# Expert stage of a two-layer transformer step: 16 base tiles and 9 overflow tiles replaced by 10 full tiles and 8 passes of two 64-row halves

## The chip, the cores and the metric

The kernel runs on one core of a Trainium2 chip. The metric is device time in microseconds (us). One execution of the kernel before was also recorded by the hardware profiler; every number of the trace below is from it. Engines are called as in the profile: PE is TensorE (PEld its weight load), DVE is VectorE, ACT is ScalarE, POOL is GpSimd, SP is SyncE, which here only issues DMAs.

## The reference

640 tokens (128 of a prompt, 512 of a sample) of width 1024 go through two layers. Each layer is attention of two kinds, gates and an output projection, and then a mixture of experts, all in float32. The part that the change touches is this:

```
scores = sigmoid(h @ w_router); sel = scores + b_router         # 16 experts in 4 groups
best   = the group whose two highest sel have the largest sum
idx    = top_k(sel inside that group, 2); w = scores[idx] / sum
out   += w * ((silu(h @ w_gate[e]) * (h @ w_up[e])) @ w_down[e])   # for both experts e of a token
```

w_gate[e] and w_up[e] are 1024x256, w_down[e] is 256x1024: 3.15 MB for one expert, 50.3 MB for the 16 of a layer. There are 2 x 640 = 1280 (token, expert) rows a layer. On the inputs that setup_inputs() draws, the reference gives these rows per expert (counted with the reference itself in float32):

```
layer 0:  76  68  88  84  55  98 112  91  75  73  65  87  48  88  73  99
layer 1:  46  13  48  31  92 153  71 104  90  41  48 115 102 112 109 105
```

## The kernel before

Each engine has its own instruction stream, written out by hand, and semaphores (class Signal) tie them together. A layer runs attention, projections, the output projection w_out, the router with its matmuls (router(t)), a block of small DVE operations that turn the scores into a place for each row (L1566 to L1618), and the expert stage. 

**Tiles.** The expert stage works in tiles of 128 rows. MOE_TILES is 25 in each layer, whatever the routing: 16 base tiles, tile e for the first 128 rows of expert e, whose weights are known ahead, and N_OVER = 9 overflow tiles for what an expert has beyond 128 rows; the expert of an overflow tile stands in etab, computed from the routing, and an unused overflow tile loads and computes expert 15's weights with rows that aren't stored. SCHED is base 0, over 0, then base, base, over, seven times, and last base, over. PE runs all 25.

**Matmuls.** In a base tile every product is done in three passes (pass3, L1792 to L1794): weights and rows are split into a high part (ACT, L809, written as fp32r) and the rest (DVE, L1157), and hi x hi, lo x hi and hi x lo are accumulated. Gate and up together are 8 x 3 matmuls of 128x512, down is 4 x 3. An overflow tile does gate and up in plain float32 from the raw data (L2128, 8 matmuls; the profile shows each float32 matmul as two records) and down in three passes, after the split of its two down units (L1064, L1539).

**PE's order** for tile n: gate_up(n); x_transposes(n + 1) (L2105, 8 transposes of the gathered rows); down(n - 1); hid_transposes(n) (L2156). After tile 0 come slot_weights (L2163, L2166), which place the routing weights. gate_up(n) waits for the rows' split (L1625), for its weights, and for PSUM bank 0, which the silu and the product of tile n - 1 read.

**DMA.** Expert weights come in six units of 512 KB from w_moe. SP issues them: weights(n, first, last) at L600 for base tiles, in 2 x 6 slots that alternate by expert, and over_weights(j) at L607 for overflow tiles, in 6 slots. Each load waits until PE has used its slot. The first base tile's six units and four of the second's are issued during w_out and the router, among the loads of the next layer's modulation weights (head_pair, raw_h). The others follow etab. POOL issues the gathers of rows, rows(n) at L765 (xg from h2_d by the indices inv_i, two buffers, two tiles ahead), and the scatters of results, store_rows(n) at L780 (ye_d from ysb by row_i). Both are indirect DMAs with a bounds check: an index beyond it is skipped. POOL's queue is in order: a gather behind a scatter waits until it is issued.

**Around it.** Before rows(0) can be gathered, the DVE block must have given inv_i (L1613). PE meanwhile runs head_pair matmuls of the next layer (layer 0 only, L1765: four matmuls side by side, each 32 output columns wide in the array, as at L1751 for mod_pair and L1720 in the prologue) and keep_busy matmuls (L1700). The neighbourhood attention's na_values (L2004) uses 64-column matmuls, two side by side. After the last tile SP loads ye_d back (L567) and DVE adds it up with the gates gt, which POOL had loaded at the end of the w_out stage; in layer 0, ACT and DVE also split the next layer's first weight units (L813, L1161), which SP loads into slots 0 to 5 as soon as the last even expert has left them.

## Time and profile before

| | |
|---|---|
| median of 3 runs | 1751.56 us (1748.84 to 1753.78) |
| profiled execution, span from first to last instruction | 1758.7 us |
| instructions | 22838 |
| PE busy | 1654.2 us, 94% |
| DVE busy | 1087.9 us, 62% |
| ACT busy | 859.0 us, 49% |
| POOL busy | 207.0 us, 12% |
| DMA | 368.02 MB, mean 209 GB/s |

A time of the profiled execution other than its span isn't given; the span lies 7.1 us above the median. Busy shares are averages over stages: PE's 94% says that it is nearly always the engine at work, and the slices say where DMA comes close to its most. A matmul's record covers its latency, so consecutive records overlap; the distance of two starts is what a matmul costs.

### The profile page before, as it was taken

The numbers are of one execution on the slowest core, as the hardware profiler recorded it, in microseconds if no ns is written. First come the engines' busy times: TensorE is split into PE (matmuls) and PEld (weight loads), VectorE is DVE, ScalarE is ACT, GpSimd is POOL, SyncE is SP. The second block draws the span as 40 slices with busy tenths as digits, with TensorE's granted clock in tenths as the row PEclk, the third lists the DMA queues.
The fourth block names the chain that finished last, engine by engine and source line by source line (L and its number), as shares of the span: only waits on it lengthen the run. The fifth ranks groups of instructions, "written<-read, shape, count | busy, mean of one in ns | idle before, by whom it ended". The sixth has DMA issues, their size and how long they took to land. (4 is left out here: it accounts for less than half of the span.)

```text
span 1758.7 us, 22838 instructions
## 1 busy us (share of the span) xinstructions
PE 1654.2 (94%) x8536; PEld 1255.2 (71%) x8536; DVE 1087.9 (62%) x1917; ACT 859.0 (49%) x1537; POOL 207.0 (12%) x257
## 2 busy tenths in 40 slices
PE   4999999999999999999779999999999998999992
PEld 2777777777887677777467677777778886777771
DVE  2476655345564668787676566544655476878775
ACT  4534553355422357676553445344552233767661
POOL 1000000011100112222100000001110001222210
PEclk9999999999999999999989999999999999999996
DMA  8531234434636699999635411453436536899975
GB/s 342 211 126 43 72 106 161 148 108 153 217 127 270 250 338 355 382 353 371 218 141 185 172 42 61 146 200 107 154 105 207 215 115 233 313 380 356 385 295 207
DMA packets 106780, 368.02 MB, mean 209 GB/s; under 512 B 20384, under 2 KB 20448, under 8 KB 106160
## 3 DMA queue, kind: packets, MB, share of 16 engines
q1 hardware_dynamic: 76752, 279.48, 43.3%
q0 software_dynamic: 29776, 84.48, 13.7%
q10 hardware_dynamic: 144, 2.62, 0.4%
q8 instruction: 68, 1.11, 0.3%
q14 instruction: 40, 0.33, 0.1%
HBM read 347.03 MB, written 49.45 MB: 225 GB/s over the span
## 5 line engine op out<-in xcount | busy, mean ns | idle before, releaser
L1157 DVE TENSOR_TENSOR lo<-raw,hi 128x1024 fp32r<-128x1024 f32 x298 | 352.2, 1218 | 104.4 <-ACT hi L809 104.2
L1792 PE MATMUL ps<-hi,hT_hi 128*128 128x512 f32 x960 | 395.2, 412 | 5.5 <-ACT o_a L1012 3.0
L1794 PE MATMUL ps<-hi,hT_lo 128*128 128x512 f32 x960 | 378.8, 395 | 0.0
L1793 PE MATMUL ps<-lo,hT_hi 128*128 128x512 f32 x960 | 377.8, 394 | 0.0
L809 ACT ACTIVATE hi<-raw 128x1024 fp32r<-128x1024 f32 x298 | 299.3, 1054 | 138.9 <-DMA raw<-w_stream 135.5
L1792 PEld LDWEIGHTS ps<-hi,hT_hi 128*128 128x128 f32 x960 | 183.1, 191 | 63.5 <-issue 18.6
L1794 PEld LDWEIGHTS ps<-hi,hT_lo 128*128 128x128 f32 x960 | 182.4, 190 | 41.0
L1793 PEld LDWEIGHTS ps<-lo,hT_hi 128*128 128x128 f32 x960 | 183.5, 191 | 33.4
L2128 PE MATMUL ps<-over,xT 128*128 128x512 f32 x288 | 126.6, 592 | 0.0
L1792 PE MATMUL ps<-hi,xT_hi 128*128 128x512 f32 x256 | 103.3, 404 | 0.5 <-DVE xT_lo L1625 0.3
L780 POOL DMA_INDIRECT ye_d<-ysb,row_i x50 | 57.4, 1147 | 371.2 <-DVE ysb L1637 335.0
L1794 PE MATMUL ps<-hi,xT_lo 128*128 128x512 f32 x256 | 100.1, 391 | 0.0
L1793 PE MATMUL ps<-lo,xT_hi 128*128 128x512 f32 x256 | 100.0, 390 | 0.0
L2128 PEld LDWEIGHTS ps<-over,xT 128*128 128x128 f32 x288 | 53.3, 190 | 60.3 <-issue 60.3
L989 ACT ACTIVATE e_da<-ps,neg_m 128x640 f32<-128x640 f32 (+1 forms) x80 | 55.9, 705 | 71.6 <-DVE neg_m L1416 71.5
L1416 DVE TENSOR_REDUCE neg_m<-ps 128x1 f32<-128x640 f32 (+1 forms) x80 | 53.7, 712 | 56.9 <-PE ps L1933 38.4
L1272 DVE TENSOR_REDUCE ssum<-sq 128x8 f32<-128x512 f32 x40 | 27.3, 685 | 83.1 <-ACT stg L906 83.1
L905 ACT ACTIVATE sq<-ps 128x512 f32<-128x512 f32 x40 | 23.9, 598 | 109.3 <-PE ps L1794 109.3
L1108 ACT ACTIVATE silu_g<-ps 128x256 f32<-128x256 f32 x50 | 19.2, 384 | 108.9 <-PE ps L1794 76.2
L845 ACT ACTIVATE pT_na<-ps 128x384 f32<-128x384 f32 (+1 forms) x80 | 31.8, 447 | 78.9 <-PE ps L1784 78.8
L765 POOL DMA_INDIRECT xg<-h_d,inv_i x50 | 57.0, 1141 | 71.9 <-DVE inv_i L1613 31.9
L1099 ACT ACTIVATE ysb<-ps,w_slot 128x512 f32<-128x512 f32 x50 | 34.4, 688 | 58.8 <-PE ps L1794 58.8
(290 smaller groups left out, 2871.4 us busy)
## 6 DMA issues: line engine op xcount, KB each, us to landing
raw<-w_moe SPq DMA_DIRECT2D x192, 512.0 KB, 6.8
raw<-w_stream SPq DMA_DIRECT2D x112, 512.0 KB, 4.3
over<-w_moe SPq DMA_DIRECT2D x108, 512.0 KB, 7.8
raw_m<-w_stream SPq DMA_DIRECT2D x70, 512.0 KB, 5.3
bias_na<-na_bias POOLq DMA_DIRECT2D x32, 384.0 KB, 3.3
sg<-sg_d POOLq DMA_DIRECT2D x8, 1280.0 KB, 9.8
y<-ye_d SPq DMA_DIRECT2D x20, 512.0 KB, 7.4
raw_p<-w_stream SPq DMA_DIRECT2D x16, 512.0 KB, 16.2
```

Source lines behind the costliest of these rows:

```text
L765: po.indirect_dma_start(xg[n % 2][:], None, h2_d, bass.IndirectOffsetOnAxis(inv_i[:, XD_COL[n]:XD_COL[n] + 1], 0), bounds_check=NT * P - 1 ...
L780: po.indirect_dma_start(ye_d, bass.IndirectOffsetOnAxis(row_i[:, XD_COL[n]:XD_COL[n] + 1], 0), ysb[n % 2][:], None, bounds_check=2 * NT * ...
L809: act.activation(hi[s][:], raw[s][:], ACT.Copy).then_inc(is_hi.sem, 1)
L845: act.activation(dst, src, ACT.Copy, scale=scale).then_inc(tr_act.sem, 1)
L989: act.activation(e_da[:, i % 2, m, 0:nk], ps_flat[:, m * 1024:m * 1024 + nk], ACT.Exp, bias=neg_m[:, 2 * (i % 2) + m:2 * (i % 2) + m + 1], ...
L1099: act.activation(ysb[n % 2][:, 0:512], ps[:, 2, :], ACT.Copy, scale=w_slot[:, c:c + 1]).then_inc(y_act.sem, 1)
L1157: dve.tensor_tensor(lo[s][:], raw[s][:], hi[s][:].bitcast(F32), ALU.subtract).then_inc(is_lo.sem, 1)
L1416: dve.tensor_reduce(neg_m[:, c:c + 1], ps_flat[:, m * 1024:m * 1024 + nk], AX.X, ALU.max, negate=True).then_inc(mx_done.sem, 1)
L1792: pe.matmul(out, w_hi, m_hi, start=first, stop=False)
L1793: pe.matmul(out, w_hi, m_lo, start=False, stop=False)
L1794: return pe.matmul(out, w_lo, m_hi, start=False, stop=last)
L2128: ins = pe.matmul(ps[:, 0, :], xT[:, kc, :], over[k][:, j * 512:(j + 1) * 512], start=(kc == 0), stop=(kc == KC - 1))
```

## The change

Rows of an expert are cut in chunks of 64. Chunks go in pairs into full tiles of 128 rows; a rest of one chunk becomes a half. There are N_FULL = 10 full tiles and N_HALF = 16 halves in N_PAIR = 8 pairs: 18 tiles in each layer instead of 25. Full tiles are given out in the order of the experts until the 10 are used, and what is left goes into halves. By the counts above, layer 0 has 14 experts that need a full tile, of which 10 get one, and 10 halves; layer 1 uses 10 full tiles and 7 halves. A used half comes first: halves 0 to 9 are pairs 0 to 4, halves 0 to 6 are pairs 0 to 3.

- Full tiles are as the base tiles before, with the expert taken from etab (weights(j, units)); full tile 0 does gate and up in plain float32 from the raw data, like an overflow tile before. No weights are loaded before etab is known.
- A pair is one tile whose rows 0 to 63 are of one expert and 64 to 127 of another. Gate and up are 8 x 2 float32 matmuls, each with 64 of the rows as its 64 columns in the array and 512 moving columns, the two halves to the two halves of PSUM's partitions; down is 2 x 2 x 2 of them. Nothing of a pair is split in hi and lo.
- POOL loads a pair's weights by indirect DMA with indices eidx: pair_gate_up(q), 2 x 2.1 MB (128 rows of 16 KB each), once PE has done gate_up of the pair before, since there is one buffer for each half; pair_down(q), 4 x 0.5 MB, once down of the pair before is done. An empty half's indices are out of bounds.
- The schedule is full 0, pair 4, full 1, pair 0, full 2, pair 5, full 3, pair 1, full 4, pair 6, full 5, pair 2, full 6, pair 7, full 7, pair 3, full 8, full 9.
- The DVE block has more steps before the places are known: two counts instead of one, two running sums over the experts instead of one, what is kept of the full tiles, and the tables of the experts, which now come before the places.
- The weight tensors are laid out anew: w_gu has one row of 16 KB for each (layer, expert, partition), w_dn one of 4 KB for each (layer, half of the inner width, expert, partition).
- Two of the loads of gt move behind the last pair's down, since their place is lent to pair_dn.

```diff
-N_OVER = (2 * NT * P) // (P + 1)
-MOE_TILES = N_EXP + N_OVER
+HALF = P // 2
+CHUNKS = NT * P // HALF
+N_HALF = N_EXP
+N_FULL = -(-(N_EXP + (2 * NT * P - N_EXP) // HALF - N_HALF) // 2)
+N_PAIR = N_HALF // 2
+MOE_TILES = N_FULL + N_PAIR
+PAIRS = [i + h * (N_PAIR // 2) for i in range(N_PAIR // 2) for h in (1, 0)]
+for _j in range(N_FULL):
+    SCHED += [("full", _j)] + [("pair", i) for i in PAIRS[_j:_j + 1]]
+IS_PLAIN = [not full or n == 0 for n, full in enumerate(IS_FULL)]
...
+                def weights(j, units):
                     e = sp.value_load(etab[0:1, j:j + 1], min_val=0, max_val=N_EXP - 1)
+                    for k in units:
+                        w = mslot(j, k)
+                        sp.wait_ge(used[w].sem, used[w].at(l, mload(j, k) - 1))
+                        src = gu_rows[l, e, :, k * D:(k + 1) * D] if k < 4 else dn_rows[l, k - 4, e]
+                        sp.dma_start(raw[w][:], src.rearrange("p (a b) -> p a b", b=512)).then_inc(loaded[w].sem, 16)
+                for p in range(4, KC):
                     head_pair(p)
                 sp.wait_ge(etab_ready.sem, etab_ready.at(l, 0))
-                sp.wait_ge(h2_stored.sem, h2_stored.at(l, NT - 1))
+                weights(0, range(MU))
                 if l + 1 < DEPTH:
+                    for b in (1, 2):
+                        sp.wait_ge(h_used[b].sem, h_used[b].at(l, 1))
+                sp.wait_ge(xg_loaded[0].sem, xg_loaded[0].at(l, 0))
+                weights(1, range(MU))
                 for n in range(MOE_TILES):
+                    if IS_FULL[n] and SCHED[n][1] + 2 < N_FULL:
+                        weights(SCHED[n][1] + 2, range(4))
+                    if n >= 1 and IS_FULL[n - 1] and SCHED[n - 1][1] + 2 < N_FULL:
+                        weights(SCHED[n - 1][1] + 2, (4, 5))
...
+                def pair_gate_up(q):
+                    if q >= 1:
+                        po.wait_ge(gu_used.sem, gu_used.at(l, q - 1))
+                    for h in range(2):
+                        c = 2 * PAIRS[q] + h
+                        po.indirect_dma_start(pair_gu[h][:], None, w_gu, bass.IndirectOffsetOnAxis(eidx[:, 0, c:c + 1], 0),
+                                              bounds_check=(l + 1) * N_EXP * P - 1, oob_is_err=False
+                                              ).then_inc(gu_loaded.sem, 16)
...
                 rows(0)
+                if l + 1 < DEPTH:
+                    for b in (0, 2):
+                        po.wait_ge(h_used[b].sem, h_used[b].at(l, 1))
+                po.wait_ge(eidx_ready.sem, eidx_ready.at(l, 0))
+                pair_gate_up(0)
                 rows(1)
...
                 for n in range(MOE_TILES):
                     if n + 2 < MOE_TILES:
                         rows(n + 2)
+                    if n in PAIR_AT[:-1]:
+                        pair_gate_up(PAIR_AT.index(n) + 1)
                     if n >= 1:
                         store_rows(n - 1)
+                    if n == 1:
+                        pair_down(0)
+                    if n - 1 in PAIR_AT[:-1]:
+                        pair_down(PAIR_AT.index(n - 1) + 1)
...
+                RED(chunks[:], counted[:, :, 0:CHUNKS], AX.X, ALU.add)
+                after(chained(RED(fulls[:], counted[:, :, CHUNKS:], AX.X, ALU.add)))
+                before(fulls, f_base)
+                after(chained(TS(kept[:], f_base[:], -1.0, float(N_FULL), ALU.mult, ALU.add)))
+                after(chained(STT(out=kept[:], in0=kept[:], scalar=0.0, in1=fulls[:], op0=ALU.max, op1=ALU.min)))
+                after(chained(STT(out=chunks[:], in0=kept[:], scalar=-2.0, in1=chunks[:], op0=ALU.mult, op1=ALU.add)))
+                before(chunks, h_base)
...
+                    if kind == "pair":
+                        pe.wait_ge(gu_loaded.sem, gu_loaded.at(l, 2 * PAIR_AT.index(n) + 1))
+                        for kc in range(KC):
+                            for h in range(2):
+                                cs = slice(HALF * h, HALF * h + HALF)
+                                ins = pe.matmul(ps[cs, 0, :], xT[:, kc, cs], pair_gu[h][:, kc * 512:(kc + 1) * 512],
+                                                start=(kc == 0), stop=(kc == KC - 1))
+                        ins.then_inc(gu_used.sem, 1)
+                        return
```

## Rows read from the trace of the kernel before

**Rows 1.** A stretch of layer 0's expert stage: busy us, granted clock, DMA share, GB/s.
```profile
core 0: us, PE busy (x) PEld busy (x) DVE busy (x) ACT busy (x) POOL busy (x), PEclk, DMA share, GB/s
700.00:780.00 80.00, 80.00 (x354) 59.44 (x353) 61.68 (x73) 55.89 (x80) 19.40 (x18) 1.00 0.96 370
```
**Rows 2.** PE's timeline, start and us: first transposes and last matmul of each stage.
```profile
615.52 1.42 PE L2105 MATMUL ps<-ident,xg 128*128 128x128 f32 x8 [1.84 <-DMA xg<-h_d,inv_i]
...
868.30 0.39 PE L1794 MATMUL ps<-over_hi,hidT_lo 128*128 128x512 f32 x1
...
1476.90 1.97 PE L2105 MATMUL ps<-ident,xg 128*128 128x128 f32 x8 [3.45 <-DMA xg<-h_d,inv_i]
...
1728.36 0.39 PE L1794 MATMUL ps<-over_hi,hidT_lo 128*128 128x512 f32 x1
```
**Rows 3.** PE's timeline across three tiles in the middle of layer 0.
```profile
673.54 1.03 PE L2105 MATMUL ps<-ident,xg 128*128 128x128 f32 x8
...
682.95 1.03 PE L2105 MATMUL ps<-ident,xg 128*128 128x128 f32 x8
...
686.79 7.03 PE L2128 MATMUL ps<-over,xT 128*128 128x512 f32 x16
693.66 1.04 PE L2105 MATMUL ps<-ident,xg 128*128 128x128 f32 x8
```
**Rows 4.** PE's timeline: matmuls of 32 columns, four side by side, and what follows.
```profile
35.67 1.92 PE L1720 MATMUL ps<-raw_p,c_act 128*32 128x512 f32 x16
...
945.48 0.39 PE L1794 MATMUL ps<-hi,hT_lo 128*128 128x512 f32 x1
945.80 1.06 PE L1751 MATMUL ps<-raw_m,c_act 128*32 128x512 f32 x8
946.80 0.50 PE L1792 MATMUL ps<-hi,hT_hi 128*128 128x512 f32 x1
947.13 0.39 PE L1793 MATMUL ps<-lo,hT_hi 128*128 128x512 f32 x1
```
**Rows 5.** PE's timeline: matmuls of 64 columns, two side by side.
```profile
403.61 0.66 PE L2004 MATMUL ps<-pT_na,v_sh 128*64 128x128 f32 x8
...
404.42 0.88 PE L1784 MATMUL ps<-ident,p_na 128*128 128x128 f32 x6
```
**Rows 6.** DVE's timeline: scores to places, layer 0, and the last step in layer 1.
```profile
602.25 0.23 DVE L1585 TENSOR_TENSOR nb<-ps,rc 128x64 f32<-128x64 f32 x1 [0.52 <-PE ps L2084]
...
603.23 0.42 DVE L1590 TENSOR_REDUCE base_s<-nb 128x16 f32<-128x256 f32 x1
...
604.43 0.24 DVE L1594 TENSOR_TENSOR slot<-slot,rc 128x80 f32<-128x80 f32 x1
...
608.84 0.18 DVE L1613 TENSOR_SCALAR inv_i<-ps 128x25 int32<-128x25 f32 x1 [0.39 <-PE ps L2093]
...
1466.92 0.18 DVE L1613 TENSOR_SCALAR inv_i<-ps 128x25 int32<-128x25 f32 x1 [0.38 <-PE ps L2093]
```
**Rows 7.** Line L765 (ns min/median/max; us to landing), and PE's timeline of filler matmuls before them.
```profile
L765 POOL DMA_INDIRECT xg<-h_d,inv_i x50: 985/1106/2114, 609.9 to 1696.9; - x50
...
DMA to landing us min/median/max: 3.3/7.8/9.3
...
603.07 4.15 PE L1700 MATMUL ps<-rope_c,ident 128*128 128x256 f32 x18
```
**Rows 8.** DMA queues by packets, MB and share of 16 engines; DMA issues, us to landing.
```profile
q0 software_dynamic: 29776, 84.48, 13.7%
...
bias_na<-na_bias POOLq DMA_DIRECT2D x32, 384.0 KB, 3.3
...
x<-x_in POOLq DMA_DIRECT2D x1, 2560.0 KB, 13.4
x_spill<-x POOLq DMA_DIRECT2D x1, 2560.0 KB, 9.8
...
tok<-tok_in POOLq DMA_DIRECT2D x1, 5.0 KB, 9.6
```

More of the change, by code:

```diff
@@ L446, in program @@
         etab_ready = Signal("etab_ready", 1)
+        eidx_ready = Signal("eidx_ready", 1)
         half = [(MOE_TILES + 1 - b) // 2 for b in range(2)]
@@ L1590, in _ @@
-                after(chained(RED(base_s[:], nb[:], AX.X, ALU.add)))
-                after(chained(STT(out=base1[:], in0=base_s[:], scalar=float(P), in1=con["c15"], op0=ALU.mult, op1=ALU.add)))
-                after(chained(STT(out=slot[:], in0=place, scalar=float(P), in1=bc_t(base1[:]), op0=ALU.is_ge, op1=ALU.mult)))
+                counted = nb[:, :, 0:CHUNKS + CHUNKS // 2]
+                after(chained(TT(counted, total.unsqueeze(2).to_broadcast([P, N_EXP, CHUNKS + CHUNKS // 2]),
+                                 con["steps"].unsqueeze(1).to_broadcast([P, N_EXP, CHUNKS + CHUNKS // 2]), ALU.is_gt)))
@@ new lines, in _ @@
+                for i, (c0, c1) in enumerate(((0, N_FULL), (N_FULL, N_FULL + N_HALF))):
+                    ins = TT(ecmp[:, c0:c1, :], con["iota_t"][:, c0:c1].unsqueeze(2).to_broadcast([P, c1 - c0, N_EXP]),
+                             ends[:, i, :].unsqueeze(1).to_broadcast([P, c1 - c0, N_EXP]), ALU.is_ge)
+                after(chained(ins))
+                after(chained(RED(etab_f[:], ecmp[:], AX.X, ALU.add)))
+                TS(etab[:], etab_f[:, 0:N_FULL], float(N_EXP - 1), None, ALU.min).then_inc(etab_ready.sem, 1)
@@ new lines, in gate_up @@
+                    for k in range(4):
+                        w = mslot(i, k)
+                        if IS_PLAIN[n]:
+                            pe.wait_ge(loaded[w].sem, loaded[w].at(l, mload(i, k)))
+                        else:
+                            pe.wait_ge(is_lo.sem, is_lo.at(l, msplit(i, k)))
+                        for j in range(2):
+                            kc = 2 * k + j
+                            if IS_PLAIN[n]:
+                                ins = pe.matmul(ps[:, 0, :], xT[:, kc, :], raw[w][:, j, :], start=(kc == 0), stop=(kc == KC - 1))
+                            else:
```

332 lines of the change are left out of this document (154 added, 178 removed).

## The prediction

> **What bounds the kernel now.** I read the table of stretches first: in the middle of the expert stage of layer 0 PE is busy for 80.00 of 80 us at the full clock (2.4 GHz), while DMA stands at a share of 0.96 and 370 GB/s [rows 1]; layer 1 is alike. So PE sets the pace, and DMA is so near its most that whatever shortens PE meets it. Then PE's timeline gives the length of the two stages, from the first transposes to the last matmul: 868.69 - 615.52 = 253.2 us in layer 0, 1728.75 - 1476.90 = 251.9 us in layer 1 [rows 2]. The distance of the transposes of neighbouring tiles is the price of a tile: 9.41 us for a base tile, 10.71 us for one with an overflow tile's float32 gate and up [rows 3]. 16 x 9.41 + 9 x 10.71 = 247 us, which leaves 5 to 6 us for the two ends: the stage is the sum of its tiles, with no stall in it. The time to be won or lost is therefore 25 tiles against 18, at prices that PE sets, as long as the weights come in time.
>
> **The price of a tile in parts.** The overflow tile's gate and up take 693.66 - 686.79 = 6.87 us, 0.859 us for each of 8 float32 matmuls [rows 3]. A base tile has 24 passes in their place and costs 1.30 us less, so a pass is 5.57 / 24 = 0.232 us, and what is neither gate, up nor down is 9.41 - 36 x 0.232 = 1.06 us.
>
> **A pair.** It has 12 rounds (8 for gate and up, 4 for down) of two float32 matmuls in different halves of the array's columns. Before has four such matmuls side by side, 32 columns each: one round of four takes 1.06 us, two rounds 1.92 us [rows 4], so a round costs 0.86 us, as much as one full-width float32 matmul. They run at the same time. Going in and out of this mode costs 0.09 + 0.11 + 0.10 = 0.3 us beyond the matmuls' own (945.48 to 945.80 is 0.32, 945.80 to 946.80 is 1.00 against about 0.89, 946.80 to 947.13 is 0.33, with 0.23 normal) [rows 4]; a pair does it twice. Pair: 12 x 0.86 + 0.6 + 1.06 = 12.0 us. No row shows two 64-column float32 matmuls that stream 512. The nearest are na_values': 12 passes with their weight loads in 0.81 us [rows 5], at most 0.07 us a load, 0.27 us a round if none were hidden. So a pair lies between 12.0 and 12.0 + 12 x 0.27 = 15.2; I take 12.0, since in the rounds of four the loads were hidden. The Trainium skill (TensorEngine Tiling (Array Packing), Key Properties) says that changing the tiling mode drains the engine, which speaks against a stage that changes it four times a pair; the 0.3 us above is that drain as this trace has it, so the rule is in the sum already.
>
> **PE's sum.** Of 16 base tiles 9 remain as full tiles, and full 0 costs what an overflow tile costs. Gone are 7 base tiles and 8 overflow tiles, new are 8 pairs: -7 x 9.41 - 8 x 10.71 + 8 x 12.0 = -55.6 us a layer, -111 us for both.
>
> **DVE, ACT, POOL.** Splits fall from 114 to 56 units a layer, by the code, so DVE and ACT have more room than before in tiles that are as long. POOL issues per full tile and pair 4 gathers and scatters and 6 weight loads. Its cost for an indirect load of 16 KB rows isn't shown; an indirect DMA of 4 KB rows takes 1.1 us of POOL [rows 7], and even with four times that for the two of 16 KB rows the cycle's POOL work is 8 x 1.1 + 2 x 4.4 = 17.6 us of 21.4. Empty halves load nothing, if indices out of bounds are skipped: the software queue moved 84.48 MB, its direct DMAs (34 groups of issues, first and last shown) come to 63.5 MB, and the remaining 21.0 MB are just 2 x 2 x 1280 rows of 4 KB; the unused rows of 25 tiles moved nothing [rows 8].
>
> **The start of the stage.** The DVE block gets longer before the places are known. By size, 25 elements cost 0.18 us, 80 cost 0.24, 256 cost 0.42 [rows 6], about 1 ns for each further element, and 0.04 between two. Before, the eight steps from the count to slot took 604.67 - 602.25 = 2.4 us [rows 6]. After there are 24: ten of 16 elements (1.8), four of 256 and two of about it (2.5), four of 80 (1.0), a reduction of 416 (0.6), two counts (0.6), 160 compared (0.3), and gaps (0.8), 7.6 us in all. That is +5.2, and -0.2 for smaller tables. inv_i (609.0 in layer 0 [rows 6]) moves to about 614.0. This is on the path. What follows gets shorter: a gather takes 3.3 us at least and 7.8 in the median [rows 7], and it now meets only the loads of full 0 (3.1 MB, begun some 6 us earlier, as etab comes first) instead of a full queue. PE had its first rows 6.5 us after inv_i in layer 0 and 9.8 us in layer 1 [rows 2, 6]; I expect 5 in both. PE's filler ends at 607.2 [rows 7] and would wait until 612.6 for the places; after such an idle stretch (3.45 us) the eight transposes took 1.97 us instead of 1.04 [rows 2, 3], so about 1 us more. Together +5 us for both layers (3 to 8). No weights are preloaded now, but full 0's start at etab (about 607.7) and take 8.5 us at 370 GB/s, so that they are there at about 617, before its rows: nothing; at two thirds of that rate 3 us are lost, the upper end of the 8.
>
> **DMA.** Full tiles 31.5 MB, halves 31.5 MB in layer 0 and 22 MB in layer 1, rows 10.5 MB: 73.5 and 64 MB against 89 before. At 0.37 MB/us [rows 1] that is 199 and 173 us, beside 197.6 us of PE (253.2 - 55.6). So it fits on average, barely in layer 0; what matters is when. Gate and up of a pair have one buffer. Its 4.19 MB can start when PE is through with gate_up of the pair before and are wanted a cycle less that gate_up later: 9.41 + 12.0 - 8 x 0.86 = 14.5 us. POOL's big direct DMAs took 9.8 and 13.4 us for 2.62 MB [rows 8]; 4.19 MB at those rates are 15.7 and 21.5 us, so 1 to 7 us are missing. The wait stands on PE before gate_up; behind it are the transposes, down and thus ys of the tile before. This occurs only for pairs that are loaded and not the first: 4 in layer 0, 3 in layer 1 (pair 3 there has one half, 2.1 MB, which fits). I take 2 us, the rate of the quicker row, since every second pair is empty and leaves the queue idle: 7 x 2 = 14 us (7 to 49). Layer 0's first pair is loaded too, with rows(1) behind it in POOL's queue and full 1's 3.1 MB beside: 7.9 MB from about 617 end at 638, gate_up of full 0 at about 628. If POOL's go first, 6 us are lost, between 0 and 11. Such idle stretches cost PE its clock for a moment, about half a us each and more after the longest: 4 us (0 to 10).
>
> **The end.** SP can load the next layer's first six units only once full 8 has left slots 0 to 5, 16 to 9 us before the last matmul; 3.1 MB are 8.5 us. Nothing, by this cover. The last tile ends as before.
>
> **Sum.** 1758.7 - 111 + 5 + 14 + 6 + 4 = 1676.7 us of span; the profiled execution lies 7.1 us above the median, so 1669.6: I say 1670. The low end leaves out all stalls and takes 3 for the start, 1643; I put it at 1640. The high end has 49 + 11 + 10 of stalls and clock, 8 for the start, and a third of the unhidden loads (1 us a pair, 16): 1758.7 - 111 + 94 - 7.1 = 1735.
>
> **The rivals.**
> First, *the queues share alike*. In the 14.5 us SP also has 1.05 MB (down units) and 2.1 MB (gate and up of a later full tile) to load, none of it urgent. If the indirect load gets no more than its equal part, it ends when all 7.3 MB are moved, at 0.37 MB/us 19.8 us: 5.3 us missing, 7 x 3.3 = 23 us more than I take, and some 4 more at the start of layer 0: 1697. For it speaks that in before a gather of 0.5 MB took 7.8 us in the median [rows 7] beside SP's loads; against it, that the 16 KB rows may weigh more than SP's 4 KB rows, and that SP's queue is empty half the time. The Trainium skill (DMA: Bandwidth & Descriptors, Queues, rings and completion order) says that each DMA engine goes round between its queues packet by packet, which with packets of equal size is this rival. Chance 0.22.
> Second, *no two at once*. If two 64-column float32 matmuls don't run side by side, a pair costs 24 x 0.859 + 0.6 + 1.06 = 22.3 us, 16 x 10.3 = 165 us more, with the load waits hidden (-24): 1670 + 165 - 24 = 1811, slower. It decides from 18.6 us a pair, where 8 pairs and 2.5 us of start make up for the 7 x 9.41 + 8 x 10.71 = 151.6 us that go. Four 32-column ones do run together [rows 4]; only the width is new. 0.07.
> Third, *the indirect loads are slow*. If the software queue can't do better than a gather and a scatter in 7.8 us (1.05 MB, 0.134 MB/us [rows 7]), gate and up take 31 us and 17 are missing each time; with down's 2.1 MB and the rows in the same queue two cycles need 63 us instead of 43: 1670 + 20 x 7, with layer 0's start 20 instead of 6 and the 14 already in my sum taken off, 1810, slower. Against it: the direct DMAs of the same queue [rows 8]. 0.08.
> Fourth, *a mixture worse than my bounds* (slow issue on POOL, the clock, late units of full tiles), 1735 to 1760: 0.08.
>
> **How the numbers follow.** My case has 0.55. The range 1640 to 1735 holds it and the first rival and leaves out the others and a little of each side: about 0.77. A measurement of this kernel can tell about 0.3% (5 us) from no change. Faster by more: 0.55 + 0.22 + half of the fourth, 0.81; within: 0.04; slower: 0.15.
>
> **What would show it.** Transposes of a full tile and its pair 21.4 us apart where the pair is empty; gate_up of a pair about 6.9 us long, its records of the two column halves at nearly one start; if 13.7, the second rival. PE waiting before gate_up of loaded pairs for pair_gu by DMA, 1 to 7 us, seven times; if near 17, the third. inv_i 5.0 us later after the count. DMA moving 63 + 10.5 and 53.5 + 10.5 MB in the stages. What would make me wrong most easily is the wait for pair_gu, of which no row tells the rate.

## The result, and the profile after

The changed kernel takes 1760.3 us in the median (1750.44 to 1766.16), the kernel before 1753.01 us: a ratio of 1.0043, 95% interval 1.0032 to 1.0053. It is slower by a little more than can be told from no change. The prediction said 1670 us, 5% faster.

The profile page of the changed kernel: the span, the busy time of each engine, the two main DMA queues, and the two groups of a pair's matmuls (last column: PE's idle time before them, and what ended it).

```profile
span 1751.6 us, 21782 instructions
...
PE 1558.7 (89%) x8212; PEld 1116.4 (64%) x8212; DVE 922.6 (53%) x1747; ACT 715.5 (41%) x1351; POOL 291.6 (17%) x325
...
q1 hardware_dynamic: 50832, 185.10, 29.7%
q0 software_dynamic: 39568, 137.96, 21.4%
...
L2169 PE MATMUL ps<-pair_gu,xT 128*64 128x512 f32 x512 | 126.4, 651 | 41.5 <-DMA pair_gu<-w_gu,eidx 41.5
...
L2210 PE MATMUL ps<-dn_a,hidT 128*64 128x512 f32 x128 | 63.3, 641 | 32.3 <-issue 32.3
```

Read it as a balance. PE's busy time fell from 1654.2 to 1558.7, by 95.5 us; its idle time (span less busy) rose from 104.5 to 192.9, by 88.4 us; the difference is the 7.1 us by which the two profiled spans differ. Of the idle time that came, 41.5 us stand before a pair's gate and up, 32.3 before a pair's down. The software queue moved 84.48 MB before [rows 8] and now 53.5 MB more, which is what the loaded halves hold and no more: empty halves do load nothing.

PE's timeline, start and duration, with the idle time before a row in brackets. Both ends of each stage, the stretch of the first pairs of layer 0, a full tile and an empty pair (752.47 to 773.92), and the first down of layer 1.

```profile
620.31 1.09 PE L2153 MATMUL ps<-ident,xg 128*128 128x128 f32 x8 [1.08 <-DMA xg<-h_d,inv_i]
...
634.08 1.97 PE L2153 MATMUL ps<-ident,xg 128*128 128x128 f32 x8 [4.81 <-DMA xg<-h_d,inv_i]
...
675.07 1.08 PE L2210 MATMUL ps<-dn_a,hidT 128*64 128x512 f32 x1 [18.43 <-issue]
675.08 1.12 PE L2210 MATMUL ps<-dn_b,hidT 128*64 128x512 f32 x1
...
681.47 0.44 PE L2218 MATMUL ps<-ident,hid 128*128 128x128 f32 x2
681.84 7.09 PE L2169 MATMUL ps<-pair_gu,xT 128*64 128x512 f32 x32
...
710.18 1.09 PE L2153 MATMUL ps<-ident,xg 128*128 128x128 f32 x8
...
733.41 9.75 PE L2169 MATMUL ps<-pair_gu,xT 128*64 128x512 f32 x32 [7.89 <-DMA pair_gu<-w_gu,eidx]
...
752.47 1.03 PE L2153 MATMUL ps<-ident,xg 128*128 128x128 f32 x8
...
773.92 1.03 PE L2153 MATMUL ps<-ident,xg 128*128 128x128 f32 x8
...
876.43 0.39 PE L1842 MATMUL ps<-hi,hidT_lo 128*128 128x512 f32 x1
...
1483.85 1.04 PE L2153 MATMUL ps<-ident,xg 128*128 128x128 f32 x8
...
1526.28 1.08 PE L2210 MATMUL ps<-dn_a,hidT 128*64 128x512 f32 x1 [13.91 <-issue]
...
1720.01 0.39 PE L1842 MATMUL ps<-hi,hidT_lo 128*128 128x512 f32 x1
```

The stages now last 876.82 - 620.31 = 256.5 us and 1720.40 - 1483.85 = 236.6 us, against 253.2 and 251.9 [rows 2]. Two things are to be seen. A pair's gate and up take 7.02 us at the full clock (681.84 to 688.86), and the two column halves start together (in the down, 675.07 and 675.08): the pair is as cheap as forecast. And behind each long wait the work is slower: 9.75 us for the same gate and up at 733.41, 6.40 us for the down at 675.07, which takes 3.59 in the next pair.

PE's waits for loads over 2 us are 4.81, 18.43, 7.89, 7.79 and 7.56 us in layer 0 and 13.91, 7.64, 7.81 and 2.79 in layer 1. With three under 1 us they come to 80.7 us; the 1.08 us ahead of the stage's first rows aren't counted.

What POOL did meanwhile, from its timeline: it issues all loads of pairs and rows, one after another, into one queue.

```profile
647.14 0.99 POOL L783 DMA_INDIRECT pair_gu<-w_gu,eidx  x1 [9.33 <-PE ps L2169]
...
652.97 1.02 POOL L793 DMA_INDIRECT dn_a<-w_dn,eidx  x1 [0.31 <-issue]
...
704.52 1.00 POOL L813 DMA_INDIRECT ye_d<-ysb,row_i  x1 [6.53 <-DVE ysb L1687]
705.84 1.13 POOL L793 DMA_INDIRECT dn_a<-w_dn,eidx  x1 [0.30 <-issue]
707.27 1.95 POOL L793 DMA_INDIRECT dn_b<-w_dn,eidx  x1 [0.30 <-issue]
709.52 1.96 POOL L793 DMA_INDIRECT dn_a<-w_dn,eidx  x1 [0.31 <-issue]
711.79 0.99 POOL L793 DMA_INDIRECT dn_b<-w_dn,eidx  x1 [0.30 <-issue]
713.09 0.99 POOL L773 DMA_INDIRECT xg<-h_d,inv_i  x1 [0.30 <-issue]
714.39 0.99 POOL L783 DMA_INDIRECT pair_gu<-w_gu,eidx  x1 [0.30 <-issue]
```

The down weights of the first pair are issued at 652.97, behind the 4.2 MB of the second pair's gate and up (647.14), and PE waits for them until 675.07. In the loop, PE left the gate/up buffer at 710.18, but the next load goes out at 714.39: a store, four down issues (8 us with their gaps) and the rows stand ahead of it. By the schedule these four belong to pair 5, which is empty in layer 0: they move nothing, and the trace has the DMA engines at a share of 0.03 from 708.4 to 713. The two other loads that are waited for in layer 0 look alike: the buffer is free at 764.40 and 816.65, the load is issued at 768.60 and 820.87, again behind the down issues of an empty pair.

The stretches around the first stall, with the granted clock, the DMA share and GB/s as the last three columns:

```profile
core 0: us, PE busy (x) PEld busy (x) DVE busy (x) ACT busy (x) POOL busy (x), PEclk, DMA share, GB/s
...
646.00:656.00 10.00, 10.00 (x52) 8.21 (x51) 2.74 (x6) 2.63 (x6) 5.44 (x6) 1.00 0.72 271
656.00:675.00 19.00, 0.64 (x6) 0.40 (x4) 1.65 (x2) 2.22 (x4) 2.57 (x3) 0.61 0.98 391
675.00:690.00 15.00, 14.93 (x59) 5.49 (x60) 7.37 (x8) 6.52 (x9) 5.88 (x4) 0.81 0.25 92
...
712.00:734.00 22.00, 13.50 (x63) 8.45 (x64) 10.14 (x12) 9.06 (x13) 11.83 (x10) 0.88 0.91 344
```

The DMA engines are full while PE waits (0.98) and nearly idle right after (0.25), where before had 0.96 over 80 us with PE never waiting [rows 1]. The granted clock falls to 0.61 in the wait and is 0.81 in the stretch behind it.

### The profile page after: what moved, and what is told of

It reads as the page before. It is cut to its first block, busy times and chain, and to the rows that moved or that the text cites. A ratio compares the mean times of both kernels' runs of the same rounds, so it can differ in the third digit from the quotient of the medians.

```text
span 1751.6 us, 21782 instructions
## 1 busy us (share of the span) xinstructions
PE 1558.7 (89%) x8212; PEld 1116.4 (64%) x8212; DVE 922.6 (53%) x1747; ACT 715.5 (41%) x1351; POOL 291.6 (17%) x325
## 3 DMA queue, kind: packets, MB, share of 16 engines
q0 software_dynamic: 39568, 137.96, 21.4%
## 4 chain that ended last, share of the span: by engine, by line
PE 76%; DMA 10%; DVE 5%; issue 5%; POOL 2%; ACT 2%; SPq 1%; POOLq 0%; DVEq 0%; ACTq 0%
PE ps L1840 16%; PE ps L1842 16%; PE ps L1841 16%; DMA pair_gu<-w_gu,eidx 6%; PE ps L1832 5%; PE ps L2169 5%; PE ps L1992 2%; PE ps L2210 2%; PE ps L1974 2%; PE ps L1799 2%; PE ps L2052 2%; PE ps L1748 1%; PE ps L2026 1%; PE ps L2153 1%; DMA raw_m<-w_stream 1%
## 5 line engine op out<-in xcount | busy, mean ns | idle before, releaser
L1192 DVE TENSOR_TENSOR lo<-raw,hi 128x1024 fp32r<-128x1024 f32 x218 | 258.4, 1221 | 101.0 <-ACT hi L852 100.5
L852 ACT ACTIVATE hi<-raw 128x1024 fp32r<-128x1024 f32 x218 | 219.0, 1054 | 133.2 <-DMA raw<-w_stream 133.1
L1841 PEld LDWEIGHTS ps<-lo,hT_hi 128*128 128x128 f32 x960 | 181.9, 189 | 32.3
L2169 PE MATMUL ps<-pair_gu,xT 128*64 128x512 f32 x512 | 126.4, 651 | 41.5 <-DMA pair_gu<-w_gu,eidx 41.5
L2169 PEld LDWEIGHTS ps<-pair_gu,xT 128*64 128x64 f32 x512 | 40.4, 150 | 116.7 <-issue 116.7
L1713 DVE TENSOR_TENSOR hid<-ps,silu_g 128x256 f32<-128x256 f32 x36 | 15.3, 424 | 163.4 <-ACT silu_g L1143 151.9
L2210 PE MATMUL ps<-dn_a,hidT 128*64 128x512 f32 x128 | 63.3, 641 | 32.3 <-issue 32.3
L813 POOL DMA_INDIRECT ye_d<-ysb,row_i x36 | 38.1, 1058 | 205.6 <-DVE ysb L1687 191.2
L1134 ACT ACTIVATE ysb<-ps,w_slot 128x512 f32<-128x512 f32 x36 | 24.8, 688 | 108.9 <-PE ps L2210 69.1
L1687 DVE TENSOR_SCALAR ysb<-ps,w_slot 128x512 f32<-128x512 f32 x36 | 27.0, 750 | 71.6 <-PE ps L2210 49.0
L2210 PE MATMUL ps<-dn_b,hidT 128*64 128x512 f32 x128 | 63.3, 641 | 0.0
```

The source lines that it names most:

```text
L813: po.indirect_dma_start(ye_d, bass.IndirectOffsetOnAxis(row_i[:, XD_COL[n]:XD_COL[n] + 1], 0), ysb[n % 2][:], None, bounds_check=2 * NT * ...
L852: act.activation(hi[s][:], raw[s][:], ACT.Copy).then_inc(is_hi.sem, 1)
L1192: dve.tensor_tensor(lo[s][:], raw[s][:], hi[s][:].bitcast(F32), ALU.subtract).then_inc(is_lo.sem, 1)
L1841: pe.matmul(out, w_hi, m_lo, start=False, stop=False)
L2169: ins = pe.matmul(ps[cs, 0, :], xT[:, kc, cs], pair_gu[h][:, kc * 512:(kc + 1) * 512], start=(kc == 0), stop=(kc == KC - 1))
L2210: ins = pe.matmul(ps[cs, 2 + c, :], hidT[:, k, cs], pair_dn[h][k][:, c * 512:(c + 1) * 512], start=(k == 0), stop=(k == 1))
```

## The experiments

The theory: TensorE's gain is as forecast and is given back as waits for the pairs' loads and as slow clock behind them. The rivals: the loads' volume against the order in which they are issued, SP's loads beside them, a fixed delay of indirect loads, and a clock that falls for another reason. All edits are to the changed kernel, whose 1760.3 us is what they are held against; each ratio is to the kernel before, measured beside it. The changed kernel's 20 runs spread over 16 us, and its profiled execution (span 1751.6 us) is among the quick ones. So wins read between profiled spans are smaller than those between medians: 13.6, 18.6, 7.0 and 11.7 us for the second, third, fifth and sixth kernel below, where the medians give 24.7, 25.2, 13.5 and 18.6.

**Without most of the pair loads.**

```diff
-                                              bounds_check=(l + 1) * N_EXP * P - 1, oob_is_err=False
+                                              bounds_check=(l + 1) * N_EXP * P - 1 if q < 2 else 0, oob_is_err=False
...
-                                                  bounds_check=(2 * l + k + 1) * N_EXP * P - 1, oob_is_err=False
+                                                  bounds_check=(2 * l + k + 1) * N_EXP * P - 1 if q < 2 else 0, oob_is_err=False
```

> The changed kernel, but from the third pair of a layer on no pair weights are loaded (the gathers are issued with a bound that lets no row through); the first two pairs are loaded as before, later pairs compute with what lies in the buffers, so their weights are left out. Theory A (PE's gain of 111 us is there and was given back to waits for the pairs' weights and to the slow clock behind each): the six waits for gate/up weights from the third pair on (41.5 us in the changed kernel) and the slow matmuls behind them (about 12 us) go, the waits of the second pass of each layer for its down weights (18.4 and 13.9 us) stay: 1760 - 41.5 - 12 = about 1706 us, 0.973 of the kernel before. Rival B (the waits have a cause that is not the volume of the pair loads, such as the row order of the queue or the stores in it): the issues are all still there, so the waits stay and the time stays above 1745 us.

1710.37 us, 0.9746 (0.9718 to 0.9774). Theory A within 5 us. The page's rows show the six waits at zero and those at down as they were:

```profile
L2169 PE MATMUL ps<-pair_gu,xT 128*64 128x512 f32 x512 | 113.4, 595 | 0.0
L2210 PE MATMUL ps<-dn_a,hidT 128*64 128x512 f32 x128 | 63.0, 639 | 31.8 <-issue 31.8
```

The matmuls of a gate and up also fell from 126.4 to 113.4 us in sum, with the same 512 of them: 13.0 us of slow clock, which came with the six waits.

**First pair's down ahead.**

```diff
+                    if n == 1:
+                        po.wait_ge(ws_done.sem, ws_done.at(l, 0))
+                        pair_down(0)
                     if n in PAIR_AT[:-1]:
                         pair_gate_up(PAIR_AT.index(n) + 1)
...
-                    if n == 1:
-                        pair_down(0)
```

> The changed kernel with the first pair's down weights issued ahead of the second pair's gate/up weights, instead of behind them. Theory A1 (the order in the one software queue makes the waits of 18.4 and 13.9 us: 2.1 MB, or nothing in layer 1, stand behind 4.2 MB): both waits go and nothing takes their place: 1760 - 32 - 7 for the clock = about 1721 us, 0.982. Theory A2 (the rate is what counts: the second pair's gate/up weights are needed one full-tile product later anyway and land no earlier): the wait moves to the second pair's gate/up, and only the down product of the first pair (3.5 us a layer) gets out of the way: 1751 to 1757 us, 0.999 to 1.002.

1735.59 us, 0.9891 (0.9863 to 0.9919): between the two, so neither form was right by itself.

```profile
666.56 9.33 PE L2170 MATMUL ps<-pair_gu,xT 128*64 128x512 f32 x32 [5.78 <-DMA pair_gu<-w_gu,eidx]
...
646.00:656.00 10.00, 10.00 (x50) 8.03 (x49) 2.74 (x6) 2.44 (x6) 4.27 (x5) 1.00 1.03 421
...
L2170 PE MATMUL ps<-pair_gu,xT 128*64 128x512 f32 x512 | 132.1, 675 | 52.5 <-DMA pair_gu<-w_gu,eidx 52.5
L2211 PE MATMUL ps<-dn_a,hidT 128*64 128x512 f32 x128 | 58.4, 599 | 0.0
```

The wait did move to the second pair's gate and up, but 18.43 us became 5.78 there, and 13.91 became 4.15. Of 73.8 us of waits for pairs 52.5 are left. What A2 missed is in the stretch from 646 to 656: the DMA engines' share was 0.72 there and is 1.03 now. The down weights used time of the DMA engines that had gone to waste: their issues stand at 637.86 to 646.25 now, where POOL had issued nothing between 637.81 and 647.14.

**SP's loads held back.**

```diff
+                    if IS_FULL[n] and n + 1 in PAIR_AT:
+                        sp.wait_ge(gu_loaded.sem, gu_loaded.at(l, 2 * PAIR_AT.index(n + 1) + 1))
                     if IS_FULL[n] and SCHED[n][1] + 2 < N_FULL:
                         weights(SCHED[n][1] + 2, range(4))
```

> The changed kernel with one wait more on SP: the loads of the full tile after next (four of gate/up) are issued only when the gate/up weights of the pair that follows have landed. No byte is left out. Theory A3 (the pair loads are late since SP's loads take half of the DMA engines' time beside them): gate/up weights of a pair land about 4 us sooner, the waits of 7.8 us fall to about 4, with less of the slow clock: 1735 to 1745 us. Rival (the software queue has its own limit, and what stands beside it does not count): the waits stay at 7.8 us and the time stays at 1760 us, or grows if the full tiles' weights now come late.

1735.10 us, 0.9889 (0.986 to 0.9918). A3 in direction and total. The waits in the loop fell to 5.07 to 6.29 us, less than expected, those at the first down to 14.86 and 8.88. So SP's transfers beside them were worth some 2 us to each wait in the loop, 3.6 and 5.0 at the first downs, and PE had no wait for a full tile's weights in exchange.

**Half of the bytes.**

```diff
-                        po.indirect_dma_start(pair_gu[h][:], None, w_gu, bass.IndirectOffsetOnAxis(eidx[:, 0, c:c + 1], 0),
+                        po.indirect_dma_start(pair_gu[h][:, 0:2048], None, w_gu.rearrange("r (a n) -> (r a) n", a=2),
+                                              bass.IndirectOffsetOnAxis(eidx[:, 0, c:c + 1], 0),
...
-                                ins = pe.matmul(ps[cs, 0, :], xT[:, kc, cs], pair_gu[h][:, kc * 512:(kc + 1) * 512],
+                                ins = pe.matmul(ps[cs, 0, :], xT[:, kc, cs], pair_gu[h][:, (kc % 4) * 512:(kc % 4 + 1) * 512],
```

> The changed kernel with half the bytes in each gate/up load of a pair: 8 KB a row instead of 16 KB, in as many instructions; the products of the second four row blocks use the first half again, so half of the pairs' gate/up weights is left out. Theory A (volume over a shared rate): a load of 4.2 MB took about 17.7 us from issue to landing, one of 2.1 MB 8 to 10 us, so the waits of 7.8 us go wholly, the two at the start of the layers fall from 18.4 and 13.9 to 8 or less, and the slow clock with them: 1690 to 1705 us, 0.964 to 0.973. Rival (a fixed delay of the software queue, from the issue and the descriptors of 128 rows, not from the bytes): the waits shrink by less than 2 us each and the time stays above 1742 us.

1706.48 us, 0.9737 (0.9712 to 0.9762), by theory A to 1.5 us, but not wait by wait: those in the loop shrank from 7.8 to between 2.4 and 3.3 and didn't go (that of the pair with one half from 2.79 to 0.99), those at the first down to 14.46 and 9.03. 2.1 MB less brought 5 us a wait, 0.41 MB/us. The 17.7 us from the last gate/up issue (715.69) to the landing (733.41) are thus about 10 us for its own 4.2 MB, an estimate from that rate, and 7 us for what was moved beside it: from 713.0 to 733.4 the trace has 4.88 MB on the software queue, the rows among them, and 2.44 MB on SP's. No weights stood in front, since the four down issues ahead of it are those of an empty pair.

**Work for PE while it waits.** The 30 fillers (keep_busy) stand in front of the wait for the first pair's down weights, the 16 in front of the waits for gate and up.

```diff
+                    if kind == "pair" and PAIR_AT.index(n) in (3, 5, 7):
+                        keep_busy(16, 0)
...
+                    if n == 1:
+                        keep_busy(30, 2)
```

> The changed kernel with idle products put where TensorE waits: 16 matmuls of 256 columns (0.43 us each at the full clock, 6.9 us) ahead of the gate/up of the 4th, 6th and 8th pair of each layer, and 30 (12.9 us) ahead of the first pair's down. Nothing else differs; the waits for the loads end when they ended. Theory C (the products behind a wait run at the 1.2 GHz level because TensorE stood idle before: the first down took 6.9 us instead of 3.5, the gate/ups of pairs 8.5 to 9.75 us instead of 7.09): with TensorE kept at work they take their full-clock time; 2 x 3.4 + 12.3 us are won, 4.1 us are lost where the wait was only 2.8 us: 1760 - 15 = about 1745 us. Rival (the lower clock comes from elsewhere, such as the loads that run then): the products stay slow and the time is 1760 to 1766 us.

1746.77 us, 0.9966 (0.9954 to 0.9978): theory C within 2 us. PE's timeline at the fourth pair's gate and up, the one at 733.41 above, and the stretch from 712 to 734:

```profile
724.79 7.07 PE L1748 MATMUL ps<-rope_c,ident 128*128 128x256 f32 x32
732.45 7.09 PE L2171 MATMUL ps<-pair_gu,xT 128*64 128x512 f32 x32 [0.59 <-DMA pair_gu<-w_gu,eidx]
...
712.00:734.00 22.00, 21.37 (x101) 14.72 (x102) 10.15 (x12) 9.06 (x13) 12.32 (x11) 1.00 0.90 343
```

With the filler the granted clock stays at 1.00, the 2.4 GHz level, where it was 0.88 with part of the stretch at 1.2 GHz, and the gate and up take 7.09 us instead of 9.75, beside the same DMA traffic (0.90 against 0.91). Over all pairs gate and up fell from 126.4 to 114.5 us in sum. The Trainium skill (TensorE: Matmul & The Clock Gate, HAM oscillation — how this bites in real kernels) describes a loop that waits for a transfer in each turn and so pays the slow clock in each turn. The trace agrees: without fillers each of the six waits has slower matmuls behind it.

**Gate and up in two halves.**

```diff
+                    for part in range(2):
+                        if q >= 1:
+                            free = (gu_half, gu_used)[part]
+                            po.wait_ge(free.sem, free.at(l, q - 1))
...
+                            if kc == 4:
+                                ins.then_inc(gu_half.sem, 1)
+                                pe.wait_ge(gu_load2.sem, gu_load2.at(l, 2 * PAIR_AT.index(n) + 1))
```

> The changed kernel with each gate/up load of a pair in two halves (the first four row blocks and the second four, each with its own semaphores): the first half is released 3.5 us earlier, and TensorE starts when it has landed. Same bytes, two more issues per pair on GpSimd (2.6 us). Theory A (the wait is the landing time of 4.2 MB over a shared rate): the first half lands 8 to 9 us sooner, when TensorE comes, and the second is waited for about 4.4 us instead of 7.8: six times 3.4 us, and some of the slow clock, 1735 to 1742 us; the waits at the start of the layers stay, since they are for the down weights. Rival (GpSimd's issue order sets the time, not the bytes): the four issues of a pair come behind the same down issues and 2.6 us later, nothing is won, 1757 us or more.

1741.71 us, 0.9933 (0.9911 to 0.9955), at the upper end of theory A. The page has 29.3 us of waits before gate and up instead of 41.5, and 29.3 before down. A wait of 7.9 became two, of 2.7 and 2.6 us.

**Rows moved.**

```diff
+                rows(1)
                 po.wait_ge(eidx_ready.sem, eidx_ready.at(l, 0))
                 pair_gate_up(0)
-                rows(1)
...
-                    if n + 2 < MOE_TILES:
-                        rows(n + 2)
                     if n in PAIR_AT[:-1]:
                         pair_gate_up(PAIR_AT.index(n) + 1)
+                    if n + 2 < MOE_TILES:
+                        rows(n + 2)
```

> The changed kernel with the gathers of token rows moved: the second tile's rows ahead of the first pair's gate/up weights, and in the loop the rows of the tile after next behind the pair's gate/up issue instead of ahead of it. Theory: the wait of 4.8 us for the second tile's rows in layer 0 goes (with about 1 us of slow clock), and six gate/up loads are issued 1.3 us sooner, so their waits fall from 7.8 to 6.5: 1760 - 6 - 8 = about 1746 us. Rival (the rows now stand behind 4.2 MB of weights and come late themselves, so that what is won there is lost at the transposes): 1758 us or more.

1822.89 us, 1.0407 (1.0377 to 1.0437): my theory missed by 77 us. The rival (1758 us or more) was right, though it gave no idea of the size.

```profile
734.38 1.97 PE L2153 MATMUL ps<-ident,xg 128*128 128x128 f32 x8 [14.05 <-DMA xg<-h_d,inv_i]
...
716.14 0.99 POOL L773 DMA_INDIRECT xg<-h_d,inv_i  x1 [0.30 <-issue]
...
L2153 PE MATMUL ps<-ident,xg 128*128 128x128 f32 x288 | 47.9, 320 | 121.9 <-DMA xg<-h_d,inv_i 121.9
L2169 PE MATMUL ps<-pair_gu,xT 128*64 128x512 f32 x512 | 113.4, 595 | 1.4 <-DMA pair_gu<-w_gu,eidx 1.4
```

Rows of 0.5 MB, issued at 716.14 right behind 4.2 MB of weights, are there at 734.38. They came to be waited for by 121.9 us in all, while gate and up, which the move was to help, waited 1.4. This is the clearest sight of what the first down suffers from: what is issued on this queue lands behind what was issued before it. The Trainium skill (DMA: Bandwidth & Descriptors, Queues, rings and completion order) says of the queues of SP and ACT that each DMA engine consumes descriptors in the order of its ring. This run shows the same order on POOL's software queue.

**All orders together.**

Its edit is those of four kernels above: first pair's down ahead, SP's loads held back, gate and up in two halves, rows moved. In the loop they read together:

```diff
+                    if n == 1:
+                        po.wait_ge(ws_done.sem, ws_done.at(l, 0))
+                        pair_down(0)
+                    if n in PAIR_AT[:-1]:
+                        pair_gate_up(PAIR_AT.index(n) + 1)
                     if n + 2 < MOE_TILES:
                         rows(n + 2)
-                    if n in PAIR_AT[:-1]:
-                        pair_gate_up(PAIR_AT.index(n) + 1)
                     if n >= 1:
                         store_rows(n - 1)
-                    if n == 1:
-                        pair_down(0)
```

> All the reorderings together, the whole computation: first pair's down weights ahead of the second pair's gate/up (it gave -25 us alone), full tiles' loads behind the pair's gate/up (-25 us alone), gate/up in two halves, token rows as in the run beside this one. Theory A (TensorE's work for a layer is as short as forecast, and only waits for the pairs' loads stand in its way): the waits left are 3 to 4 at the start of a layer and 0 to 2 per pair, some 15 us in all with little of the slow clock: 1680 to 1695 us, 0.958 to 0.967 of the kernel before, faster than both. Rival (the DMA engines' rate as a whole is the limit, so that the gains overlap and cancel): no better than the best one alone, 1730 us or more.

1786.41 us, 1.0187 (1.0164 to 1.0209). Theory A missed it by over 90 us; the rival's number is met, but not for its reason. The moved rows spoiled it: seven transposes wait 11 to 18 us for their rows. The next kernel leaves that one edit out.

**The same with the rows in the loop kept in front.**

Against the kernel with all orders:

```diff
+                    if n + 2 < MOE_TILES:
+                        rows(n + 2)
                     if n == 1:
                         po.wait_ge(ws_done.sem, ws_done.at(l, 0))
                         pair_down(0)
                     if n in PAIR_AT[:-1]:
                         pair_gate_up(PAIR_AT.index(n) + 1)
-                    if n + 2 < MOE_TILES:
-                        rows(n + 2)
```

> The kernel with all orders changed, but with the token rows in the loop back ahead of the gate/up issue, as in the changed kernel; only the second tile's rows stay ahead of the first pair's weights. The whole computation. Theory (the software queue lands in order, so 0.5 MB of rows behind 4.2 MB of weights cost 12 to 14 us each, and nothing else spoiled the run with all orders): the waits are those of the single edits less what they saved: 25 + 25 + 19 us with some overlap, 1695 to 1710 us, 0.966 to 0.975, faster than both kernels. Rival (the edits draw on the same 20 us of the DMA engines' time): 1725 to 1735 us.

1695.65 us, 0.9667 (0.965 to 0.9684), at the theory's lower end and faster than both kernels.

```profile
PE 1548.9 (91%) x8212; PEld 1111.5 (66%) x8212; DVE 922.6 (54%) x1749; ACT 715.7 (42%) x1351; POOL 326.6 (19%) x357
...
L2183 PE MATMUL ps<-pair_gu,xT 128*64 128x512 f32 x512 | 118.2, 610 | 16.3 <-DMA pair_gu<-w_gu,eidx 16.1
...
L2224 PE MATMUL ps<-dn_a,hidT 128*64 128x512 f32 x128 | 58.3, 598 | 1.9 <-issue 1.9
```

Waits for pairs are down from 73.8 to 18.2 us. The gains of the single edits (25, 25, 19) nearly added up, to 65 (between profiled spans 13.6, 18.6 and 11.7 came to 57.9, more than their sum): they mend different stretches.

**Only one pair's weights loaded.**

```diff
-                        c = 2 * PAIRS[q] + h
+                        c = (2 * PAIRS[q] if q else 0) + h
...
-                                              bounds_check=(l + 1) * N_EXP * P - 1, oob_is_err=False
+                                              bounds_check=(l + 1) * N_EXP * P - 1 if q < 1 else 0, oob_is_err=False
```

> The changed kernel in which only the first pair of each layer loads its weights (those of experts 0 and 1) and every later pair computes with them, so the weights of all other pairs are left out. It measures what the stage takes when TensorE waits for no pair weights. By the prediction's sum without its waits for gate/up weights (14) and for the clock (4): 1652 us. By the trace of the changed kernel, less its waits for pair weights (41.5 + 32.3) and the slow clock behind them (about 20): 1666 us. If TensorE's part of the gain had been smaller than forecast, 1680 us or more.

1699.91 us, 0.9689 (0.9668 to 0.971). All three numbers were missed, since the experiment doesn't do what I wrote: the first pair's down weights are still issued late, and 22.0 us of waits for them (11.11 and 10.89) remain with none of the second pair's weights ahead of them in their queue. That is of use too: of the 18.43 us in layer 0 about 11 come from the late issue and from the 2.1 MB themselves, beside SP's loads, about 7 from standing behind the second pair. For the price of PE's work it has to be read by stages, below.

**Down ahead of the store.**

```diff
+                    if n - 1 in PAIR_AT[:-1]:
+                        pair_down(PAIR_AT.index(n - 1) + 1)
                     if n >= 1:
                         store_rows(n - 1)
-                    if n - 1 in PAIR_AT[:-1]:
-                        pair_down(PAIR_AT.index(n - 1) + 1)
```

> The fastest kernel so far (1695.65 us, 0.9667) with one thing more: GpSimd issues a pair's down weights ahead of the store of the rows of the pair before, so these and the gate/up weights behind them go out 1.3 us sooner plus what the store waits for its rows (1.5 us). The whole computation. Theory (the issue times on GpSimd still count: down issues of 8 us stand ahead of the gate/up issue): the remaining waits of about 2 us at the pairs' gate/up shrink by 1 to 2 us each in seven places, 1683 to 1690 us. Rival (the volume is the limit where pairs with rows are loaded, DMA share 0.97 to 1.00 there): no change, 1693 to 1698 us, or later stores delay the end.

1703.78 us, 0.9711 (0.9674 to 0.9749), no gain; it lies 8 us above the kernel it was to improve, with intervals that touch. The waits before gate and up are 14.7 us against 16.3, so the theory's gain is there in kind and small; what costs the rest I didn't find, and it stays open.

**The second tile's rows ahead, alone.**

```diff
+                rows(1)
                 po.wait_ge(eidx_ready.sem, eidx_ready.at(l, 0))
                 pair_gate_up(0)
-                rows(1)
```

> The changed kernel with the second tile's rows issued ahead of the first pair's gate/up weights, and nothing else. The wait of 4.8 us for these rows in layer 0 (in layer 1 there is none) goes; the first pair's gate/up, landed 1.3 us later, is waited for by 1.4 us as in the run that had this edit and the other order of rows: 1760 - 3.4 - 1 for the clock = about 1755 to 1757 us. Rival (the start is limited by the volume of all loads, so that the gain is lost at the next wait, the first pair's down): 1759 to 1761 us. If the slowdown of the run with both row orders came from this edit and not from the one in the loop: 1790 us or more.

1753.13 us, 1.0002 (0.9985 to 1.0019). The trace speaks for the rival: the wait of 4.81 us is gone, but gate and up then wait 2.17 us and the first down 20.68 instead of 18.43, the waits over 1 us come to 79.8 us against 79.7, and the span is 1751.6 us in both. Yet the median is 7 us lower, below both ranges, and the intervals of the two ratios don't overlap (0.9985 to 1.0019, and 1.0032 to 1.0053 for the changed kernel). So the runs speak for a win of some 7 us and the two traces for none. The changed kernel's runs spread over 16 us, and its profiled one is 7 us below their median; which of the two holds is open. That it didn't slow the run with both row orders is settled.

## Why the prediction was wrong, point by point

**PE's sum** (-55.6 us a layer) was right. Take from the stages of the changed kernel their waits, 48.0 and 32.7 us, and the surplus of slow gate/ups, downs and transposes over their usual 7.09, 3.59 and 1.04 us, 10.4 and 7.8 us: 198.1 and 196.1 us are left, where the sum has 253.2 - 55.6 = 197.6 and 251.9 - 55.6 = 196.3. The run with one pair loaded gives the same, by stages of 221.6 and 215.7 us less waits of 20.2 and 15.5 and slow clock of about 3.7 and 2.8: 197.7 and 197.4. A full tile and an empty pair take 21.45 us (752.47 to 773.92), forecast 21.4. So the rival *no two at once* falls.

**The start** came out near its total (3.6 us, forecast 5), in part by luck. inv_i is ready at 613.18 us in layer 0, forecast 614.0, but the first rows came 7.1 us behind it, forecast 5. PE's first rows thus came 4.8 us later than before, and the gap from the end of that stage to the first rows of layer 1 is 1.2 us shorter, where the prediction's terms give +3.5 and +0.2, and 1 us for slow transposes. The two misses cancel.

**The wait for gate and up** was mis-sized: seven of 2 us said, six of 41.5 us in all measured. The second pair of either layer is not among the six, because its weights landed while PE stood before the first pair's down. The pair with one half, which I had taken to fit, waited 2.79 us. What failed is "can start when PE is through with gate_up": the two loads went out 4.2 and 5.5 us later, behind POOL's store, down issues and rows. I had summed POOL's work over a cycle (17.6 us of 21.4, so it fits) and never asked what it does at the moment when the buffer comes free. That the transfer itself came near, 17.7 us against 16.5, is luck: I had priced 4.2 MB alone, and about 7 of the 17.7 us are other traffic. Of the 7.89 us of a wait the late issue thus explains up to 5.5, by the timeline. No run puts the load ahead of the four down issues alone, so this share is argued and not shown; the run with down ahead of the store moved them least, and took 1.6 us off all waits for gate and up together.

**The first pair's down** isn't in the sum at all, and cost 32.3 us. This is a term put at nothing without a reason. I walked through the queue for rows(1) behind pair_gate_up(0), which was right in layer 0 (6 said, 4.81 measured), and not for pair_down(0) behind pair_gate_up(1), two lines on. The run that swaps these two shows it: no wait before down is left, and 5.78 and 4.15 us stand before gate and up instead. In layer 1 the first pair is empty and loads nothing, and PE waited 13.91 us all the same: the semaphore of an empty load comes in its place in the queue.

**The clock** was put at 4 us and took about 18 (10.4 and 7.8). My half a us for each idle stretch came from one wait of 3.45 us, behind which eight transposes took 1.97 us instead of 1.04 [rows 2]: these are too few matmuls to show the whole price. Behind each of the six waits (2.79 to 7.89 us) the gate and up are slower by 1.4 to 2.7 us. The run with fillers, in which they take 7.09 us beside the same traffic, shows that the idle time is the cause.

**The rivals.** *The queues share alike* was partly true: taking SP's loads away from beside the pair's was worth 2 us a wait, of the 3.3 I had priced it with. *Indirect loads slow* is out: 4.2 MB in 17.7 us with SP's loads beside are 0.24 MB/us, against 0.134, and the run with half the bytes gives 0.41. What happened is nearest to the fourth, *a mixture*, whose price of 1735 to 1760 ends where the measurement lies; it had 0.08.

**The balance.** The forecast's span was 1676.7 us, the measured one 1751.6: 74.9 us more, of which 27.5 are gate and up, 32.3 down and 14 the clock. The last step added 15.8 us by itself: I took 7.1 us off because the profiled execution of before lay above its median, and that of the changed kernel lies 8.7 below. The two spans differ by -7.1 us, the medians by +7.3. A sum from one profiled execution carries that much, whatever its terms.

## What to carry to other kernels

When work is moved to a queue that lands in order, write down its order of issues across two whole turns, put the bytes beside each, and read off for every consumer what stands in front; an average of the queue's or the issuing engine's load says nothing of this. Price a stall twice, once for its length and once for the slow clock behind it. And if a change frees an engine but the gain doesn't show, look for the stretch in which the DMA engines are idle though somebody waits later: here four changes of order, without a byte less, turned 0.4% slower into 3.3% faster.

## What the runs showed of the hardware

- Two float32 matmuls of 64 columns run side by side through a stream of 512: 7.02 us for eight rounds, 0.15 us more than eight at full width (6.87 us [rows 3]). So the weight loads cost at most 0.15 us in eight rounds.
- An indirect load whose indices are all out of bounds moves nothing but still completes in its turn: PE waited 13.91 us for four of them behind 4.2 MB.
- An indirect load of 128 rows of 16 KB costs POOL 0.99 us, no more than one of 4 KB; the forecast had bounded it at 4.4. Of four down issues in a row the middle two took 1.95 us each in the loop (707.27 and 709.52), though they moved nothing; the first pair's four, which moved 2.1 MB, took 0.99 to 1.02 us (652.97 on). What makes the difference stays open.
